# Two chunks of low parts on GpSimd and six on VectorE, in place of three and five, in two norms between stages

## The chip, the cores and the metric

One Trainium2 chip, one of its cores. The metric is the device time of one execution in microseconds (us). The engines are TensorE (PE, whose weight loads are listed apart as PEld), VectorE (DVE), ScalarE (ACT), GpSimd (POOL) and the queue that issues the weight loads from memory (SP).

## What is computed

Three blocks of a small network run one after the other on 256 tokens of width 1024: a mixer block with sparse attention and a gated feed-forward, a block with a convolution and Fourier mixer and a squared-ReLU feed-forward (this one also on 256 context tokens), and a block with neighbourhood attention and a squared-ReLU feed-forward. Between the stages stand norms with a shift and a gain that come from a conditioning vector:

```python
def _rms(x, g):
    xf = x.astype(jnp.float32)
    y = xf * lax.rsqrt(jnp.mean(xf * xf, axis=-1, keepdims=True) + EPS)
    return y.astype(x.dtype) * g

def _modulate(h, shift, scale):
    return h * (1 + scale) + shift
...
x = x + gx2 * _mlp(_modulate(_rms(x, norm_mlp_g[i]), sx2, cx2), mlp_w1[i], mlp_w2[i])
```

Two of these norms matter here: m0, ahead of the feed-forward of the second block, and na, ahead of the projection to queries, keys and values of the third. Both are made for 512 columns, 256 tokens and 256 context tokens side by side.

## The kernel before

**Split numbers.** A product in float32 is made of three products in a rounded format (fp32r): high part of the weights by high part of the activations, high weights by low activations, low weights by high activations. So each weight tile and each activation tile is held as a high part (a copy into fp32r) and a low part (what is left after the high part is subtracted). ScalarE copies the weights' high parts (whi, L1077), VectorE subtracts for their low parts (wlo, L1537).

**A norm that ends in split numbers.** The width of 1024 is eight chunks c = 0 to 7 of 128 partitions, each with two halves q of 256 columns. For m0 and na the order is:

1. VectorE makes the normed values of all eight chunks, half by half, into xn (L1996, 16 instructions). One operand, the inverse roots, lies in PSUM (ps[5]).
2. ScalarE adds the shift and rounds, into the high part Ahi (L1102, 16 instructions).
3. The low part is xn + shift - Ahi. GpSimd makes it for the chunks in LOW_P in two instructions a half: the subtraction (L2280, xn from xn and A) and the shift (L2282, A from xn). VectorE makes it for the other chunks in one instruction a half (L1988), after the sixteen of step 1.

```python
        def shifted_lo(st, layer, which):
            for c in LOW_P:
                for q in range(2):
                    x = xn[c][:, half(q)]
                    w.wait_ge(S(st + "_hi"), 2 * c + q + 1)
                    e.tensor_tensor(x, x, plain(Ahi[:, c, half(q)]), SUB).then_inc(own.sem, own.up())
                    w.wait_ge(own, own.n)
                    e.tensor_scalar(Alo[:, c, half(q)], x, 1.0, ada[:, layer, q, 24 * which + c:24 * which + c + 1],
                                    MUL, ADD).then_inc(S(st + "_lp").sem, 1)
```

**The first two output chunks of the next stage** (first_two, for w1_0a after m0 and for na_in after na). TensorE runs both outputs, here called tile 0 and tile 1, together over the high parts k = 0 to 7 (L589, L591), since these come one by one. Only then come the eight products with the low parts of tile 0, and then the eight of tile 1 (L595), in the order of k. Before each of tile 0, TensorE waits for both halves of low part k. Tile 0 is 512 columns wide in both stages, tile 1 is 512 in w1_0a and 256 in na_in. The other output chunks follow in `linear`, 24 matmuls each (L551, L563, L565). After na_in's tile 1 there stand first two more groups: head_sum (L950, which needs the squares that ScalarE makes of tile 0, L1469 and then L1472) and a sum for the modulation (L647).

**What each engine has behind these.** VectorE: the low parts of the weights of output chunks 2 and 3 (two times L1537), and in m0's stage two partial sums for the modulation (L1612). GpSimd: in w1_0a the squares and low parts of the hidden values (L2294, L2178), in na_in the Newton steps of the head norms (L2308). ScalarE: weights' high parts (L1077), then the outputs of tile 0 (L1367 in w1_0a). SP: loads of 512 KB into nine buffers (L474), in order, each waiting until TensorE has left the buffer that it fills.

The order of instructions on each engine is written out in the program and joined by semaphores. LOW_P sets the split on GpSimd, on VectorE and in TensorE's waits (ready_low, L606); the table IN_TURN holds how many signals each norm gives on a shared semaphore.

Of the kernel before, what the change touches and what calls it, by code (L numbers as in the profile page):

```python
# [48 lines left out]

AHEAD = {"w1_0a": 3, "na_in": 3}  # L50

LOW_P = range(3)
ADA_AFTER = {"w_in": (6, 22), "w_out": (0, 48), "w_up": (2, 42)}


# [149 lines left out]
def end_of(name):  # L205
# [6 lines left out]
                 ("d1_r", 8)],  # L212
    "normed": [("nc_t", 8), ("n2_t", 8), ("m0_t", 16), ("na_t", 16)],
    "norm_hi": [("nc_hi", 8), ("n2_hi", 8), ("m0_hi", 16), ("na_hi", 16)],
    "norm_lo": [("nc_lo", 8), ("n2_lo", 8), ("m0_lo", 10), ("na_lo", 10)],
    "norm_lo_p": [("m0_lp", 6), ("na_lp", 6)],
    "early_hi": [("e0_hi", 8), ("e1_hi", 8), ("e2_hi", 8)],
    "early_lo": [("e0_lo", 8), ("e1_lo", 8), ("e2_lo", 8)],
    "square": [("n1_sq", 8), ("nx_sq", 8), ("m0_sq", 8), ("na_sq", 8), ("m1_sq", 8)],
# [67 lines left out]
def launch_program(nc, dram, out):  # L287
# [222 lines left out]
    def tensor_program(e):  # L510
# [95 lines left out]
        def ready_low(v_signal, p_signal, per):  # L606

            def wait(k):
                if k in LOW_P:
                    w.wait_ge(S(p_signal), per * (k + 1))  # L610
                else:
                    w.wait_ge(S(v_signal), per * (k + 1 - len(LOW_P)))
            return wait
# [914 lines left out]
    def vector_program(e):  # L1528
# [455 lines left out]
        def shifted_lo(st, c, x, layer, which):  # L1984
            for q in range(2):
                w.wait_ge(S(st + "_hi"), 2 * c + q + 1)
                w.wait_ge(S(st + "_t"), 2 * c + q + 1)
                e.scalar_tensor_tensor(Alo[:, c, half(q)], x[:, half(q)], ada[:, layer, q, 24 * which + c:24 * which + c + 1],  # L1988
                                       plain(Ahi[:, c, half(q)]), ADD, SUB).then_inc(S(st + "_lo").sem, 1)

        def norm_whole(st, layer, which):

            for c in range(8):
                for q in range(2):
                    w.wait_ge(S(st + "_row"), 1)
                    e.scalar_tensor_tensor(xn[c][:, half(q)], R[:, c, half(q)], G[:, layer, which, q, c:c + 1], ps[5][:, half(q)],  # L1996
                                           MUL, MUL).then_inc(S(st + "_t").sem, 1)
            for c in range(len(LOW_P), 8):
                shifted_lo(st, c, xn[c], layer, which)
# [172 lines left out]
    def gpsimd_program(e):  # L2172
# [102 lines left out]
# [9 lines that stand above are left out]
# [205 lines left out]
```

## Time and profile before

| | us |
|---|---|
| median of 3 runs | 1355.67 |
| lowest and highest | 1353.74, 1355.76 |
| the profiled execution, its own time | 1354.78 |
| its span in the trace | 1352.6 |
| TensorE busy | 1318.6 (97%) |
| VectorE busy | 826.3 (61%) |
| ScalarE busy | 595.3 (44%) |
| GpSimd busy | 433.4 (32%) |

The span runs from the first to the last instruction in the trace; some 2 us lie around it. The granted clock of TensorE is given as a share of full speed: 1.00 is 2.4 GHz and 0.50 is 1.2 GHz. Each time below is one from the start of the span. The stage of m0 lies at about 575 us, that of na at about 945 us.

### The profile page before, as it was taken

The numbers are of one execution on the slowest core, as the hardware profiler recorded it, in microseconds if no ns is written. First come the engines' busy times: TensorE is split into PE (matmuls) and PEld (weight loads), VectorE is DVE, ScalarE is ACT, GpSimd is POOL, SyncE is SP. The second block draws the span as 40 slices with busy tenths as digits, with TensorE's granted clock in tenths as the row PEclk, the third lists the DMA queues.
The fourth block names the chain that finished last, engine by engine and source line by source line (L and its number), as shares of the span: only waits on it lengthen the run. The fifth ranks groups of instructions, "written<-read, shape, count | busy, mean of one in ns | idle before, by whom it ended". The sixth has DMA issues, their size and how long they took to land.

```text
span 1352.6 us, 19992 instructions
## 1 busy us (share of the span) xinstructions
PE 1318.6 (97%) x7852; PEld 1115.1 (82%) x7852; DVE 826.3 (61%) x1265; ACT 595.3 (44%) x953; POOL 433.4 (32%) x432
## 2 busy tenths in 40 slices
PE   9999999999999999979999999999799999999999
PEld 8888888899886788768788888787577777999987
DVE  6687678899776445369544444334467766855553
ACT  5336546566563223244321234222445553766432
POOL 2352132233420001265400144111556552388300
PEclk9999999999999999989999999999899999999999
DMA  7786367845455222344434333345423221555552
GB/s 288 264 280 235 142 210 277 300 181 182 162 189 193 78 94 79 111 153 160 167 128 152 143 140 140 140 142 185 161 89 108 93 84 45 187 188 181 188 191 79
DMA packets 63965, 220.08 MB, mean 163 GB/s; under 512 B 6913, under 2 KB 10241, under 8 KB 63873
## 3 DMA queue, kind: packets, MB, share of 16 engines
q1 hardware_dynamic: 63584, 218.56, 45.9%
q8 instruction: 63, 1.03, 0.3%
q10 hardware_dynamic: 288, 0.25, 0.1%
q14 instruction: 30, 0.24, 0.1%
HBM read 217.73 MB, written 1.05 MB: 162 GB/s over the span
## 4 chain that ended last, share of the span: by engine, by line
PE 89%; DVE 4%; POOL 3%; issue 2%; ACT 1%; DMA 1%; SPq 0%; DVEq 0%; POOLq 0%; ACTq 0%
PE ps L551 22%; PE ps L565 22%; PE ps L563 22%; PE ps L541 7%; PE ps L543 4%; PE ps L629 2%; POOL xn L2280 2%; PE ps L957 1%; PE ps L984 1%; PE ps L971 1%; DVE wlo L1537 1%; PE ps L595 1%; PE ps L950 1%; POOL ssum_c L2189 1%; DMA R<-in_x 1%
## 5 line engine op out<-in xcount | busy, mean ns | idle before, releaser
L551 PE MATMUL ps<-A,whi 128*128 128x256 f32 (+2 forms) x1580 | 519.3, 329 | 2.4 <-ACT A L1318 1.7
L565 PE MATMUL ps<-A,wlo 128*128 128x256 f32 (+2 forms) x1552 | 495.7, 319 | 0.1
L563 PE MATMUL ps<-A,whi 128*128 128x256 f32 (+2 forms) x1552 | 495.4, 319 | 0.0
L1537 DVE TENSOR_TENSOR wlo<-raw,whi 128x1024 fp32r<-128x1024 f32 x305 | 393.1, 1292 | 100.4 <-ACT whi L1077 100.1
L1077 ACT ACTIVATE whi<-raw 128x1024 fp32r<-128x1024 f32 x305 | 319.8, 1051 | 289.8 <-PE ps L565 163.0
L551 PEld LDWEIGHTS ps<-A,whi 128*128 128x128 f32 x1580 | 300.2, 190 | 55.9 <-issue 27.9
L563 PEld LDWEIGHTS ps<-A,whi 128*128 128x128 f32 x1552 | 295.2, 190 | 22.3 <-issue 1.9
L565 PEld LDWEIGHTS ps<-A,wlo 128*128 128x128 f32 x1552 | 294.7, 190 | 21.2 <-DVE wlo L1537 0.4
L541 PE MATMUL ps<-H,whi 128*128 128x512 f32 x432 | 151.4, 394 | 0.0
L2178 POOL TENSOR_TENSOR H<-tmp,H 128x256 fp32r<-128x256 f32 (+1 forms) x86 | 123.9, 1440 | 63.8 <-ACT H L1372 45.8
L543 PE MATMUL ps<-H,wlo 128*128 128x256 f32 x432 | 121.4, 281 | 0.0
L565 PE MATMUL ps<-H,wlo 128*128 128x512 f32 (+1 forms) x296 | 111.1, 375 | 0.6 <-DVE wlo L1537 0.6
L551 PE MATMUL ps<-H,whi 128*128 128x512 f32 (+1 forms) x296 | 111.5, 377 | 0.0
L563 PE MATMUL ps<-H,whi 128*128 128x512 f32 (+1 forms) x296 | 110.9, 375 | 0.0
L2294 POOL TENSOR_TENSOR tmp<-tmp 128x512 f32<-128x512 f32 (+1 forms) x64 | 56.0, 876 | 157.6 <-ACT tmp L1367 157.6
L541 PEld LDWEIGHTS ps<-H,whi 128*128 128x128 f32 x432 | 81.4, 188 | 18.1
L1961 DVE SCALAR_TENSOR_TENSOR R<-ps,ada,R 128x256 f32<-128x256 f32 x56 | 24.8, 479 | 114.9 <-PE ps L565 113.9
L2189 POOL TENSOR_TENSOR ssum<-ssum,sq 128x256 f32<-128x256 f32 (+1 forms) x30 | 32.0, 1067 | 170.7 <-ACT sq L1092 170.7
L543 PEld LDWEIGHTS ps<-H,wlo 128*128 128x128 f32 x432 | 82.1, 190 | 0.1
L551 PEld LDWEIGHTS ps<-H,whi 128*128 128x128 f32 x296 | 55.7, 188 | 11.7 <-issue 0.8
L565 PEld LDWEIGHTS ps<-H,wlo 128*128 128x128 f32 x296 | 55.7, 188 | 10.8 <-DVE wlo L1537 0.8
L563 PEld LDWEIGHTS ps<-H,whi 128*128 128x128 f32 x296 | 55.7, 188 | 9.9
(282 smaller groups left out, 1461.1 us busy)
## 6 DMA issues: line engine op xcount, KB each, us to landing
raw<-in_ada SPq DMA_DIRECT2D x96, 512.0 KB, 4.3
raw<-in_w SPq DMA_DIRECT2D x64, 512.0 KB, 3.4
raw<-in_w_up SPq DMA_DIRECT2D x44, 512.0 KB, 4.2
raw<-in_w_in SPq DMA_DIRECT2D x38, 512.0 KB, 5.5
raw<-in_w_0a SPq DMA_DIRECT2D x32, 512.0 KB, 3.6
raw<-in_w_0b SPq DMA_DIRECT2D x32, 512.0 KB, 3.4
raw<-in_na_in SPq DMA_DIRECT2D x24, 512.0 KB, 5.3
raw<-in_w_down SPq DMA_DIRECT2D x22, 512.0 KB, 3.4
```

The source lines that it names most:

```text
L541: e.matmul(ps[g % 3], w_hi, both(k), start=k == 0, stop=False)
L543: m = e.matmul(o, w_lo, ah, start=False, stop=last)
L551: e.matmul(o, w_hi, ah, start=k == 0, stop=False)
L563: e.matmul(o, w_hi, al, start=False, stop=False)
L565: m = e.matmul(o, w_lo, ah, start=False, stop=last)
L629: m = e.matmul(ps[7][q:q + 32, :], cond[:, k, :], raw[slot][:, 512 * j:512 * j + 512], start=k == 0 or i in (88, 89), stop=k == 7 and i < 48)
L1077: e.activation(whi[s % NHI][:, :cols], raw[i % NRAW][:, :cols], ACT.Copy).then_inc(S("whi").sem, 1)
L1537: e.tensor_tensor(wlo[i % NRAW][:, :cols], raw[i % NRAW][:, :cols], plain(whi[s % NHI][:, :cols]), SUB).then_inc(S("wlo").sem, 1)
L2178: e.tensor_tensor(into, x, plain(hi), SUB).then_inc(S(done).sem, 1)
L2189: e.tensor_tensor(total, total, x, ADD).then_inc(S(st + "_part").sem, 1)
L2280: e.tensor_tensor(x, x, plain(Ahi[:, c, half(q)]), SUB).then_inc(own.sem, own.up())
L2294: e.tensor_tensor(x, x, x, MUL).then_inc(S(st + "_sq").sem, 1)
```

## The change

GpSimd makes the low parts of chunks 0 and 1 in place of 0, 1 and 2, and VectorE those of chunks 2 to 7 in place of 3 to 7, in both norms. The counts of signals follow: two halves for each of the 6 chunks and 2 chunks.

```diff
-LOW_P = range(3)
+LOW_P = range(2)
...
-    "norm_lo": [("nc_lo", 8), ("n2_lo", 8), ("m0_lo", 10), ("na_lo", 10)],
-    "norm_lo_p": [("m0_lp", 6), ("na_lp", 6)],
+    "norm_lo": [("nc_lo", 8), ("n2_lo", 8), ("m0_lo", 12), ("na_lo", 12)],
+    "norm_lo_p": [("m0_lp", 4), ("na_lp", 4)],
```

On VectorE, in the norm m0 (xn_126 is the normed chunk 2, xn_127 chunk 3, and so on; "x2" is the two halves), the difference of the orders reads:

```order
 L1996 SCALAR_TENSOR_TENSOR xn_130<-R,G,ps 128x256 x2
 L1996 SCALAR_TENSOR_TENSOR xn_131<-R,G,ps 128x256 x2
+L1988 SCALAR_TENSOR_TENSOR A<-xn_126,ada,A 128x256 x2
 L1988 SCALAR_TENSOR_TENSOR A<-xn_127,ada,A 128x256 x2
 L1988 SCALAR_TENSOR_TENSOR A<-xn_128,ada,A 128x256 x2
```

Two instructions are put ahead of the ten, so each of those, and what stands behind them, comes two places later; the same two rows are added in na. On GpSimd, in the norm m0 (tmp_87 is the first hidden tile of the stage that follows):

```order
 L2280 TENSOR_TENSOR xn_125<-xn_125,A 128x256
 L2282 TENSOR_SCALAR A<-xn_125,ada 128x256
-L2280 TENSOR_TENSOR xn_126<-xn_126,A 128x256
-L2282 TENSOR_SCALAR A<-xn_126,ada 128x256
-L2280 TENSOR_TENSOR xn_126<-xn_126,A 128x256
-L2282 TENSOR_SCALAR A<-xn_126,ada 128x256
 L2294 TENSOR_TENSOR tmp_87<-tmp_87 128x512
 L2178 TENSOR_TENSOR H<-tmp_87,H 128x512
```

The last four of its twelve instructions for this norm are gone, and the same four in na. The rows of TensorE, ScalarE and SP are the same before and after.

## Rows read from the trace of the kernel before

**Rows 1.** The page: busy time, share of the span and instructions of each engine.

```profile
PE 1318.6 (97%) x7852; PEld 1115.1 (82%) x7852; DVE 826.3 (61%) x1265; ACT 595.3 (44%) x953; POOL 433.4 (32%) x432
```

**Rows 2.** TensorE's waits, whole span: total us, times, longest.

```profile
PE ps L595 <- POOL A L2282: 12.7, 2, 6.5
...
PE ps L589 <- ACT A L1102: 1.7, 2, 0.8
```

**Rows 3.** Timeline of GpSimd, 566 to 602 us: start, us, what.

```profile
576.19 0.73 POOL L2280 TENSOR_TENSOR xn<-xn,A 128x256 f32<-128x256 f32 x1 [8.63 <-ACT A L1102]
...
580.92 0.48 POOL L2282 TENSOR_SCALAR A<-xn,ada 128x256 fp32r<-128x256 f32 x1
581.37 6.89 POOL L2280 TENSOR_TENSOR xn<-xn,A 128x256 f32<-128x256 f32 x1
...
590.38 0.48 POOL L2282 TENSOR_SCALAR A<-xn,ada 128x256 fp32r<-128x256 f32 x1
```

**Rows 4.** Timeline of VectorE, 566 to 602 us.

```profile
581.36 4.04 DVE L1988 SCALAR_TENSOR_TENSOR A<-xn,ada,A 128x256 fp32r<-128x256 f32 x10
585.32 2.35 DVE L1537 TENSOR_TENSOR wlo<-raw,whi 128x1024 fp32r<-128x1024 f32 x2
587.59 2.10 DVE L1612 TENSOR_SCALAR modsum<-raw,cond 128x1024 f32<-128x1024 f32 x2
```

**Rows 5.** Timeline of TensorE, 566 to 602 us.

```profile
583.92 0.39 PE L591 MATMUL ps<-A,wlo 128*128 128x512 f32 x1
584.14 0.61 PE L595 MATMUL ps<-A,whi 128*128 128x512 f32 x2
590.91 6.29 PE L595 MATMUL ps<-A,whi 128*128 128x512 f32 x14 [6.15 <-POOL A L2282]
597.04 0.39 PE L551 MATMUL ps<-A,whi 128*128 128x512 f32 x1
```

**Rows 6.** Timeline of GpSimd, 936 to 972 us.

```profile
951.43 6.86 POOL L2280 TENSOR_TENSOR xn<-xn,A 128x256 f32<-128x256 f32 x1
...
959.66 0.48 POOL L2282 TENSOR_SCALAR A<-xn,ada 128x256 fp32r<-128x256 f32 x1
```

**Rows 7.** Timeline of VectorE, 936 to 972 us.

```profile
951.39 4.04 DVE L1988 SCALAR_TENSOR_TENSOR A<-xn,ada,A 128x256 fp32r<-128x256 f32 x10
```

**Rows 8.** Timeline of TensorE, 936 to 990 us.

```profile
947.39 0.28 PE L589 MATMUL ps<-A,whi 128*128 128x256 f32 x1
947.50 0.28 PE L591 MATMUL ps<-A,wlo 128*128 128x256 f32 x1
...
953.05 0.63 PE L595 MATMUL ps<-A,whi 128*128 128x512 f32 x2
960.19 4.63 PE L595 MATMUL ps<-A,whi 128*128 128x512 f32 x14 [6.51 <-POOL A L2282]
964.62 1.53 PE L950 MATMUL ps<-sq,con 128*128 128x512 f32 x2
...
967.08 0.50 PE L551 MATMUL ps<-A,whi 128*128 128x512 f32 x1
...
983.40 1.02 PE L950 MATMUL ps<-sq,con 128*128 128x512 f32 x2
```

**Rows 9.** Timeline of ScalarE, 936 to 972 us.

```profile
963.16 0.60 ACT L1469 ACTIVATE k<-ps 128x512 f32<-128x512 f32 x1 [9.06 <-PE ps L595]
963.65 0.59 ACT L1472 ACTIVATE sq<-ps 128x512 f32<-128x512 f32 x1
```

**Rows 10.** Stretches: us, busy time and count of each engine, granted clock, DMA share, GB/s.

```profile
670.00:760.00 90.00, 90.00 (x407) 73.07 (x407) 34.85 (x41) 18.44 (x19) 3.64 (x3) 1.00 0.39 141
590.90:597.20 6.30, 6.29 (x15) 4.97 (x16) 0.00 (x0) 0.60 (x1) 1.04 (x1) 0.52 0.26 86
960.20:965.00 4.80, 4.80 (x15) 4.18 (x16) 0.00 (x0) 1.09 (x2) 0.00 (x0) 0.50 0.16 55
```

**Rows 11.** Timeline of SP's loads, 560 to 640 us: the second of the two issues last.

```profile
573.60 20.60 SPq L474 DMA_DIRECT2D raw<-in_w_0a  x2
```

## Prediction

> **What bounds the kernel now.** I read the page first: TensorE is busy 1318.6 of 1352.6 us [rows 1], so a change gains or loses by what it does to TensorE's idle time and to its clock, and by nothing else. The list of TensorE's waits comes next. Its longest entry is exactly the place that the change touches: L595, the products with the activations' low parts, waits 12.7 us in two pieces for GpSimd's L2282 [rows 2]. That is over a third of the 34 us in which TensorE is idle at all (1352.6 - 1318.6).
>
> The timelines of the two stages say why. In the first stage GpSimd's subtraction and shift of a half take 0.73 and 0.48 us and follow each other at 1.30 us a half, four times. The fourth ends at 581.40 (580.92 + 0.48). The fifth subtraction, the first half of chunk 2, starts at 581.37 and takes 6.89 us in place of 0.73 [rows 3]. What began then is VectorE's chain of low parts, at 581.36, with two L1537 right behind it and two L1612 after those, with no gap from 581.36 to 589.69 [rows 4]. The subtraction ends at 588.26, which is 0.59 us after the last L1537 (587.67). In the second stage the same subtraction starts at 951.43 and takes 6.86 us [rows 6], again in step with VectorE's chain, which begins at 951.39 [rows 7]. So the subtraction is shut out for as long as VectorE runs instructions with both tensors in SBUF back to back. It isn't shut out by L1996, whose second tensor is in PSUM: beside these the first subtraction took its 0.73 us [rows 3].
>
> The Trainium skill bears on this ("SBUF — State Buffer", section "Who interferes with whom"): a VectorE instruction with two SBUF inputs contends with a GpSimd instruction that reads SBUF, and who issues first holds the shared pair for the whole instruction. On who contends, the trace agrees (6.89 against 0.73 us). On how long, it doesn't: by a hold of one instruction the subtraction would get its turn after 0.4 us, and the waits of 6.15 and 6.51 us would hardly be there; the sum would then be next to nothing, or slightly a loss, since VectorE gets two more instructions.
>
> TensorE meanwhile does low products 0 and 1 at 584.14 and stops; it goes on at 590.91, 0.05 us after the last L2282 [rows 3, 5]. The pause also costs clock. The fourteen products left take 6.13 us (590.91 to 597.04), 0.44 each, against 0.23 for one of this width just before (583.92 to 584.14) [rows 5]. The granted clock over them is 0.52, which is 1.2 GHz nearly throughout, and 0.50 in the second stage, against 1.00, or 2.4 GHz, in steady work [rows 10].
>
> **The change part by part: the first stage.** GpSimd loses four instructions, all behind the point at which it was shut out; its first eight stand as before and end at 581.40. VectorE gets two L1988 ahead of its ten. The ten take 4.04 us with 0.48 for one, so they start (4.04 - 0.48) / 9 = 0.396 us apart [rows 4]. Twelve of them, counted j = 0 to 11, end at 581.36 + 0.396 j + 0.48; chunk k is done with j = 2(k - 2) + 1. TensorE wants chunk k at 584.14 + 0.227 k. Chunk 2 is ready at 582.24 and wanted at 584.60, chunk 5 is ready at 584.61 and wanted at 585.28, chunk 6 ready at 585.41 and wanted at 585.51: no wait. Chunk 7 is ready at 586.20, with the 0.05 us of signal 586.25, and wanted at 585.73: a wait of 0.5 us. Tile 0 ends at 586.48, tile 1 takes 8 x 0.227 = 1.82 and ends at 588.30. There the next output chunk begins, which stood at 597.04 [rows 5]. Gain: 8.7 us. Seen otherwise, 6.15 of wait less 0.5, and 3.0 of slow clock.
>
> **The second stage.** VectorE's chain starts at 951.39 [rows 7] and TensorE's low products at 953.05 [rows 8], 1.66 us after it and not 2.78 as in the first, so here VectorE is the later one. Chunks 2, 3 and 4 come in time (chunk 4 at 953.90, wanted at 953.96). Chunk 5 comes at 954.69 against 954.19, chunk 6 at 955.48, chunk 7 at 956.28: three waits of about 0.5 us, and tile 0 ends at 956.51. Tile 1 is 256 wide, 0.115 us each (947.39 to 947.50) [rows 8]: 0.92, to 957.43. L950 needs ScalarE's squares of tile 0. Before, tile 0 ended at about 960.19 + 6 x 0.44 = 962.83 (its last six products at half clock, each as in the first stage), and ScalarE started at 963.16, 0.33 later; the squares end 1.08 after that (963.65 + 0.59 - 963.16) [rows 9]. Now: 956.51 + 0.33 + 1.08 = 957.92, with the signal 957.97, a new wait of 0.5 us, formerly hidden behind tile 1 at half clock. From L950 to the next output chunk it was 967.08 - 964.62 = 2.46; L950 itself took 1.53 at the slow clock and 1.02 at the fast one, so 0.51 less: 1.95. The next output chunk begins at 959.92 in place of 967.08 [rows 8]. Gain: 7.2 us.
>
> **What else moves.** VectorE's two L1537 come 0.79 us later. The first ended at about 586.5 and now at 587.3, and TensorE wants it near 588.5 in the first stage: a cover of 1.2 us, and without it the stage would give back that much at most. GpSimd's first hidden square may now meet VectorE's chain (tile 0 is out at about 587.3, the chain with L1612 runs to 590.5) and be held up to 3 us; the hidden tiles are read only in the next product, over 70 us later, from a ring of five, so this is free. The loads: SP issued nothing from 574 to 594 and then waited on TensorE's tile 0 [rows 11], so nothing was fetched in the pause that will now be missing; these loads move forward with TensorE. The first of them is for output chunk 4, which TensorE wants two chunks (2 x 24 x 0.227 = 10.9 us) after chunk 2 begins: before at 607.9, 13.7 us behind the issue at 594.2, and now at 599.2, 12.7 us behind an issue at 586.5. One us of cover goes, since tile 1 runs at full clock, out of 13.7.
>
> **The sum.** 8.7 + 7.2 = 15.9 us. From the profiled execution's own 1354.78 that makes 1338.9 us. The median of the runs is 1355.67, 0.9 us more; I stay with the profiled one.
>
> **The bounds of what no row shows** concern the clock: whether it stays up through the three short waits in the second stage: at best nothing is lost; at worst what [rows 10] show is paid again after them (tile 1 and the last of tile 0 1.1 us, L950 0.5, and some of the next chunk, 3 us in all a stage, 6 in both). I take nothing, since the waits are 0.5 us each and TensorE already waits 0.8 us ahead of each stage's first product [rows 2] and runs the products behind that wait at 0.115 us for 256 columns, full speed [rows 8]. Upward the bound is that VectorE's twelve cost no wait at all: the waits of 6.15 and 6.51 and the slow clock, 3.0 in the first stage and in the second (964.62 - 960.19) - 6 x 0.227 - 8 x 0.115 + 0.51 = 2.7: 18.4 us, so 1336.4.
>
> **The rivals.**
> - *The clock falls in the stutter.* Up to 3 us in one stage or both: 1342 to 1345. Against it: full clock in the 90 us of steady work, and 0.8 us waits that cost nothing.
> - *Given back later.* Something after the stages is tied to time rather than to TensorE, such as a load or a norm chain. At half of the gain: 1347. For it: the attention stage has small waits of its own; against: SP's loads follow TensorE, and ScalarE had idled for 9.06 us when it got tile 0 [rows 9], so it brought no debt into the stage that follows.
> - *GpSimd is still caught.* The margin is thin: the eighth instruction ends at 581.40, VectorE's chain begins at 581.36 [rows 3, 4]. If the fourth pair is caught, it is let go at 588.26 + 0.79 = 589.05, its rest takes 0.6, and TensorE goes on at 589.7 from product 1 (15 left, 0.44 more): 0.8 us gained a stage, 1353.2. Nothing ahead of this point is altered, and both stages got through before.
> - *Slower: GpSimd is caught three pairs early.* Then the second pair is let go at 589.05, its shift takes 0.6 and two pairs follow at 1.3: chunk 1 is done at 592.25, against 590.86 for chunk 2 before, and one product more runs at half clock: 1.8 us lost a stage, 1358.5. With only the third and fourth caught it is 590.95 and 0.5 us lost a stage, 1355.9, so it decides from there on. It takes GpSimd 2.6 to 3.9 us later, or VectorE's chain that much earlier, and sixteen L1996 still stand ahead of it.
> - *The hold is one of a single instruction, and TensorE's wait has another cause.* Then VectorE's 0.79 us more a stage is all there is: 1356.4, within the measurement. Against it: TensorE goes on 0.05 us after L2282.
>
> **How the numbers follow.** Forecast 0.80 (its own range 1336.4 to 1341), clock 0.07, given back 0.06, GpSimd still caught 0.03, no hold 0.02, slower 0.02. The predicted time is 1338.9. The range takes in the clock rival and the upper bound with 0.9 us for the spread of the runs: 1335.5 to 1345. A measurement of this kernel tells 0.2%, 2.7 us, from no change. Faster by more: forecast, clock, given back and a part of the rest, 0.94; within 0.2%: 0.04; slower: 0.02.
>
> **What the profile after would show.** Right: no L2280 longer than 0.8 us, twelve L1988 in about 4.84 us, L595 waiting for VectorE's L1988 (about 0.5 us once in the first stage, 0.5 three times in the second), L595's products at 0.23 us, a clock of 1.00 in both, L950 waiting for ScalarE some 0.5 us, the next output chunk at about 588.3 and 951.2 (959.9 less 8.7). Wrong: a subtraction of over 6 us among GpSimd's eight, a clock of 0.50 behind the stutter, or a new entry of several us in TensorE's waits after 590 us.

## The result, and the profile after

| | before | after |
|---|---|---|
| median, us | 1354.7 (4 runs) | 1336.78 (4 runs) |
| lowest and highest | 1352.75, 1355.76 | 1336.65, 1338.93 |
| the profiled execution, own time | 1354.78 | 1338.93 |
| its span | 1352.6 | 1337.0 |

The changed kernel is 1.3% faster: ratio 0.9873, 95% interval 0.9856 to 0.989. The forecast was 1338.9 us.

The page after, busy times:

```profile
PE 1314.3 (98%) x7852; PEld 1111.0 (83%) x7852; DVE 825.1 (62%) x1269; ACT 595.9 (45%) x953; POOL 417.3 (31%) x424
```

Against [rows 1], GpSimd is busy for 16 us less, of which 12.3 are the time that two subtractions were held (6.89 - 0.73 and 6.86 - 0.73); TensorE is busy for 4.3 us less, mostly since its products no longer run at half clock there.

TensorE's waits after, longest first (total us, times, longest):

```profile
PE ps L675 <- POOL ssum_c L2189: 1.9, 1, 1.9
PE ps L551 <- ACT A L1318: 1.7, 3, 1.4
PE ps L711 <- ACT whi L1077: 1.5, 1, 1.5
PE ps L595 <- DVE A L1988: 1.2, 4, 0.3
```

The entry of 12.7 us [rows 2] is gone. In its place L595 waits for VectorE, four times, 1.2 us in all by this list; from start to start it is 2.2 us, as worked out below. First stage, timelines of GpSimd, VectorE and TensorE after (this execution is 1.29 us later than that of before where the norm begins, 576.38 against 575.09 for the first L1996):

```profile
577.48 0.73 POOL L2280 TENSOR_TENSOR xn<-xn,A 128x256 f32<-128x256 f32 x1 [8.64 <-ACT A L1102]
...
581.34 0.74 POOL L2280 TENSOR_TENSOR xn<-xn,A 128x256 f32<-128x256 f32 x1
582.18 0.48 POOL L2282 TENSOR_SCALAR A<-xn,ada 128x256 fp32r<-128x256 f32 x1
588.77 1.89 POOL L2294 TENSOR_TENSOR tmp<-tmp 128x512 f32<-128x512 f32 x1 [6.11 <-ACT tmp L1367]
```

```profile
576.38 6.36 DVE L1996 SCALAR_TENSOR_TENSOR xn<-R,G,ps 128x256 f32<-128x256 f32 x16 [0.76 <-PE ps L692]
582.65 4.84 DVE L1988 SCALAR_TENSOR_TENSOR A<-xn,ada,A 128x256 fp32r<-128x256 f32 x12
587.40 2.36 DVE L1537 TENSOR_TENSOR wlo<-raw,whi 128x1024 fp32r<-128x1024 f32 x2
```

```profile
585.41 1.84 PE L595 MATMUL ps<-A,whi 128*128 128x512 f32 x7
587.55 2.36 PE L595 MATMUL ps<-A,whi 128*128 128x512 f32 x9 [0.29 <-DVE A L1988]
589.75 0.40 PE L551 MATMUL ps<-A,whi 128*128 128x512 f32 x1
```

GpSimd's last shift still ends 0.01 us past the start of VectorE's chain (582.66 and 582.65) and isn't held. Seven low products run without a stop where two did [rows 5], then one gap: the eighth would start at 585.41 + 7 x 0.227 = 587.00 and starts at 587.55. The figure in brackets, 0.29, is smaller, since a matmul's span reaches past the start of the next. The hidden square L2294 met the chain and took 1.89 us; nothing waited for it. Second stage, TensorE:

```profile
945.76 1.35 PE L595 MATMUL ps<-A,whi 128*128 128x512 f32 x5
947.39 0.50 PE L595 MATMUL ps<-A,whi 128*128 128x512 f32 x1 [0.29 <-DVE A L1988]
948.19 0.50 PE L595 MATMUL ps<-A,whi 128*128 128x512 f32 x1 [0.29 <-DVE A L1988]
948.98 1.46 PE L595 MATMUL ps<-A,whi 128*128 128x512 f32 x9 [0.29 <-DVE A L1988]
950.66 1.13 PE L950 MATMUL ps<-sq,con 128*128 128x512 f32 x2 [0.22 <-ACT sq L1472]
...
952.71 0.50 PE L551 MATMUL ps<-A,whi 128*128 128x512 f32 x1
```

Three gaps while VectorE brings chunks 5, 6 and 7, and one ahead of L950. The stretches of both stages after (last three columns: granted clock, DMA share, GB/s) show full clock throughout, against 0.52 and 0.50 [rows 10]:

```profile
584.10:588.30 4.20, 3.90 (x17) 2.86 (x16) 4.20 (x10) 1.42 (x3) 0.00 (x0) 1.00 0.00 0
588.30:598.00 9.70, 9.70 (x44) 7.98 (x44) 8.96 (x8) 4.63 (x7) 5.98 (x4) 1.00 0.86 302
943.00:951.00 8.00, 6.91 (x33) 4.97 (x32) 8.00 (x17) 4.88 (x9) 1.06 (x2) 1.00 0.08 10
```

A yardstick for all runs below: the length of a stage from the first L1996 of its norm to the first L551 behind L595, read from the two timelines. Here it is 589.75 - 576.38 = 13.37 and 952.71 - 937.82 = 14.89 us; before it was 597.04 - 575.09 = 21.95 and 967.08 - 945.12 = 21.96.

### The profile page after: what moved, and what is told of

Its sections match the earlier page's. It is cut to its first block, busy times and chain, and to the rows that moved or that the text cites. A ratio compares the mean times of both kernels' runs of the same rounds, so it can differ in the third digit from the quotient of the medians.

```text
span 1337.0 us, 19992 instructions
## 1 busy us (share of the span) xinstructions
PE 1314.3 (98%) x7852; PEld 1111.0 (83%) x7852; DVE 825.1 (62%) x1269; ACT 595.9 (45%) x953; POOL 417.3 (31%) x424
## 4 chain that ended last, share of the span: by engine, by line
PE 89%; DVE 5%; ACT 2%; issue 2%; POOL 1%; DMA 1%; SPq 0%; DVEq 0%; POOLq 0%; ACTq 0%
PE ps L551 23%; PE ps L565 22%; PE ps L563 22%; PE ps L541 7%; PE ps L543 4%; PE ps L629 2%; PE ps L957 1%; PE ps L984 1%; PE ps L971 1%; DVE wlo L1537 1%; ACT A L1102 1%; PE ps L950 1%; DVE A L1988 1%; POOL ssum_c L2189 1%; DMA R<-in_x 1%
## 5 line engine op out<-in xcount | busy, mean ns | idle before, releaser
L551 PE MATMUL ps<-A,whi 128*128 128x256 f32 (+2 forms) x1580 | 519.3, 329 | 2.3 <-ACT A L1318 1.7
L565 PE MATMUL ps<-A,wlo 128*128 128x256 f32 (+2 forms) x1552 | 495.9, 320 | 0.1
L563 PE MATMUL ps<-A,whi 128*128 128x256 f32 (+2 forms) x1552 | 495.8, 319 | 0.0
L1537 DVE TENSOR_TENSOR wlo<-raw,whi 128x1024 fp32r<-128x1024 f32 x305 | 388.6, 1277 | 92.0 <-ACT whi L1077 91.4
L551 PEld LDWEIGHTS ps<-A,whi 128*128 128x128 f32 x1580 | 300.3, 190 | 55.3 <-issue 25.9
L563 PEld LDWEIGHTS ps<-A,whi 128*128 128x128 f32 x1552 | 295.6, 190 | 22.0 <-issue 1.7
L565 PEld LDWEIGHTS ps<-A,wlo 128*128 128x128 f32 x1552 | 295.1, 190 | 21.4 <-DVE wlo L1537 0.4
L565 PE MATMUL ps<-H,wlo 128*128 128x512 f32 (+1 forms) x296 | 111.1, 375 | 0.6 <-DVE wlo L1537 0.6
L551 PE MATMUL ps<-H,whi 128*128 128x512 f32 (+1 forms) x296 | 111.5, 377 | 0.0
L563 PE MATMUL ps<-H,whi 128*128 128x512 f32 (+1 forms) x296 | 111.0, 375 | 0.0
L2294 POOL TENSOR_TENSOR tmp<-tmp 128x512 f32<-128x512 f32 (+1 forms) x64 | 58.3, 911 | 159.1 <-ACT tmp L1367 158.9
L551 PEld LDWEIGHTS ps<-H,whi 128*128 128x128 f32 x296 | 55.7, 188 | 11.6 <-issue 0.8
L565 PEld LDWEIGHTS ps<-H,wlo 128*128 128x128 f32 x296 | 55.7, 188 | 10.9 <-DVE wlo L1537 0.8
L563 PEld LDWEIGHTS ps<-H,whi 128*128 128x128 f32 x296 | 55.7, 188 | 9.9
```

Source lines behind the costliest of these rows:

```text
L551: e.matmul(o, w_hi, ah, start=k == 0, stop=False)
L563: e.matmul(o, w_hi, al, start=False, stop=False)
L565: m = e.matmul(o, w_lo, ah, start=False, stop=last)
L1537: e.tensor_tensor(wlo[i % NRAW][:, :cols], raw[i % NRAW][:, :cols], plain(whi[s % NHI][:, :cols]), SUB).then_inc(S("wlo").sem, 1)
L2294: e.tensor_tensor(x, x, x, MUL).then_inc(S(st + "_sq").sem, 1)
```

## The experiments

Each was timed beside the kernel before, on three chips: runs 1 to 4, 5 to 7 and 8 to 10. All lengths are of the one profiled execution of each kernel. The expected times start from the medians of the first series, and the kernel before is 0.8 to 2.8 us lower on these chips, so a median is best read against "before, same chip".

| kernel | stage 1, us | stage 2, us | median, us | before, same chip | ratio, 95% interval |
|---|---|---|---|---|---|
| before | 21.95 | 21.96 | | | |
| the change | 13.37 | 14.89 | 1336.78 | 1354.7 | 0.9873, 0.9856 to 0.989 |
| 1 GpSimd first | 15.19 | 17.84 | 1343.31 | 1351.89 | 0.9932, 0.9909 to 0.9954 |
| 2 gaps | 16.65 | 17.76 | 1341.83 | 1351.89 | 0.9926, 0.99 to 0.9951 |
| 3 m0 alone | 13.34 | 21.38 | 1345.96 | 1351.89 | 0.9949, 0.9931 to 0.9967 |
| 4 na alone | 20.81 | 14.89 | 1343.99 | 1351.89 | 0.9945, 0.9923 to 0.9966 |
| 5 one chunk | 14.12 | 15.68 | 1339.97 | 1353.87 | 0.9895, 0.9878 to 0.9913 |
| 6 no chunk | 14.92 | 16.48 | 1342.55 | 1353.87 | 0.9915, 0.9898 to 0.9933 |
| 7 GpSimd late | 19.50 | 20.72 | 1352.46 | 1353.87 | 0.9991, 0.9978 to 1.0004 |
| 8 the change again | 13.33 | 14.89 | 1339.76 | 1353.34 | 0.99, 0.9881 to 0.9919 |
| 9 in turns | 12.64 | 14.88 | 1338.39 | 1353.34 | 0.989, 0.9871 to 0.991 |
| 10 in turns, sum first | 12.67 | 13.40 | 1337.94 | 1353.34 | 0.9879, 0.986 to 0.9899 |

**1. GpSimd first.** Is the subtraction shut out by VectorE, or slow by itself?

```diff
+            w.wait_ge(S(st + "_lp"), 6)
             for c in range(len(LOW_P), 8):
                 shifted_lo(st, c, xn[c], layer, which)
```

> The split of before (three chunks on GpSimd, five on VectorE), but VectorE waits ahead of its first L1988 until GpSimd has made all six halves. Theory 1, GpSimd is shut out by VectorE's chain: its fifth subtraction takes 0.73 us as the first four, the six halves are done 2.6 us after the fourth, VectorE's ten follow, TensorE's last low part is some 1.9 us later than with the change. Stage one gains 6.9 us and stage two 5.2 us against before: about 1342.6 us, clock 1.00 throughout. Theory 2, the fifth subtraction is slow for another reason (its data, TensorE's or ScalarE's reads of A): it takes 6.9 us again and VectorE only starts then, over 4 us lost a stage, above 1360 us.

GpSimd's fifth and sixth half, and VectorE behind them, in the first stage (L2281, L2283 are L2280, L2282 of before):

```profile
582.65 0.74 POOL L2281 TENSOR_TENSOR xn<-xn,A 128x256 f32<-128x256 f32 x1
583.49 0.48 POOL L2283 TENSOR_SCALAR A<-xn,ada 128x256 fp32r<-128x256 f32 x1
583.94 0.74 POOL L2281 TENSOR_TENSOR xn<-xn,A 128x256 f32<-128x256 f32 x1
584.77 0.48 POOL L2283 TENSOR_SCALAR A<-xn,ada 128x256 fp32r<-128x256 f32 x1
```

```profile
585.29 4.05 DVE L1988 SCALAR_TENSOR_TENSOR A<-xn,ada,A 128x256 fp32r<-128x256 f32 x10 [2.54 <-POOL A L2283]
```

The same instruction on the same data takes 0.74 us when VectorE rests, so theory 2 falls. A wait of 2.54 us put into VectorE makes the kernel faster. Stage one gained 6.76 us (6.9 expected), stage two 4.12 (5.2 expected); there the granted clock was 0.50 for some 3 us from 953.3 us on, behind six short waits of TensorE for low parts, which I hadn't reckoned with.

**2. Gaps.** How long does the hold last?

```diff
                 w.wait_ge(S(st + "_t"), 2 * c + q + 1)
+                if c > 3 or q:
+                    w.wait_ge(S(st + "_lo"), 2 * (c - 3) + q)
                 e.scalar_tensor_tensor(Alo[:, c, half(q)], ...
```

> The split of before, but each L1988 of VectorE waits until the one before it is written, so that VectorE stands still for a moment between them. Theory 1a, GpSimd is shut out only as long as VectorE's instructions overlap without a gap: the fifth subtraction gets in after one or two L1988 and takes under 2 us, the ten L1988 take 5.8 us alone and some 2 us more with GpSimd's between them, the gain is some 5 us in stage one and 4 in stage two: 1344 to 1348 us. Theory 1b, VectorE goes first whenever both want it: the subtraction lasts to the end of the chain, now 1.5 us later or more, 1356 to 1360 us.

GpSimd and VectorE in the first stage (L2282 is the subtraction here, L2284 the shift, L1990 VectorE's low part):

```profile
579.87 1.08 POOL L2282 TENSOR_TENSOR xn<-xn,A 128x256 f32<-128x256 f32 x1
581.06 0.53 POOL L2284 TENSOR_SCALAR A<-xn,ada 128x256 fp32r<-128x256 f32 x1
581.56 0.90 POOL L2282 TENSOR_TENSOR xn<-xn,A 128x256 f32<-128x256 f32 x1
582.56 0.53 POOL L2284 TENSOR_SCALAR A<-xn,ada 128x256 fp32r<-128x256 f32 x1
```

```profile
579.88 6.57 DVE L1990 SCALAR_TENSOR_TENSOR A<-xn,ada,A 128x256 fp32r<-128x256 f32 x10
```

Of the ten, the second by itself:

```profile
580.49 0.75 DVE L1990 SCALAR_TENSOR_TENSOR A<-xn,ada,A 128x256 fp32r<-128x256 f32 x1
```

Theory 1a holds. Two of VectorE's ten, the second and the fourth, started while a subtraction ran and took 0.75 us; the others took 0.48. So the ten start (6.57 - 0.48 - 2 x 0.27) / 9 = 0.62 us apart, not counting those 0.27 us, and leave 0.14 us between them, where before each began at 0.396 us, ahead of the end of the one in front (0.48 long). That is enough: the subtraction took 1.08 us beside the chain, not 6.89 [rows 3], and the two engines took turns.

The stages gained 5.3 and 4.2 us, and that with a slow clock: the granted clock was 0.50 from 586.7 to 590.1 and from 951.9 to 955.3 us. The last nine products of the first stage took 3.75 us (586.50 to 590.25) where 9 x 0.227 = 2.04 would do at full clock, so the gaps alone would be worth some 1.7 us more there (an estimate). The median of 1341.83 lies 2.2 us below the range expected; before is 2.8 us lower on this chip than on the first.

**3 and 4. One norm alone.** LOW_P by norm: two chunks for one, three for the other, with the counts of signals to match.

> Two chunks on GpSimd in the norm m0 alone, three in na as before. If the two stages pay independently and nothing is given back, the 8.6 us that the trace shows between the norm's first L1996 and the next output chunk: 1346.1 us. If what is gained in one place is given back later, clearly above that, and this run and the next don't add up to the whole.

> Two chunks on GpSimd in the norm na alone, three in m0 as before. Independent stages: the 7.1 us that the trace shows for this stage, 1347.6 us. Given back in the attention stage behind it: clearly above.

The changed stage has the same length alone as with the other (13.34 and 13.37, 14.89 and 14.89), and the stretch between the stages is 348.1 us in every kernel of the table. Behind the second stage, from its first L551 to the end of the span, it is 384.3 or 384.4 us with the change and in runs 1 to 6 and 9; in the other four (before 385.5, run 7 387.0, run 8 385.7, run 10 387.3) the clock fell somewhere in that stretch. So the two gains are independent and none is given back. The medians, 5.9 and 7.9 us below before, add up to 13.8, less sharply than the stages do; run 4 came out 3.6 us below its expectation, 1.1 of it in the stage that it left as it was. The stage left as it was came out at 20.81 and 21.38 here, not 21.95 and 21.96, with the same wait: the part at half clock varied.

**5 and 6. One chunk, no chunk on GpSimd.** The change with LOW_P one and zero chunks long.

> One chunk on GpSimd and seven on VectorE in both norms. If TensorE now waits only for the end of VectorE's chain, two more L1988 at 0.396 us put that 0.79 us later in each stage: 1.6 us slower than the change, about 1338.4 us. If the two chunks that GpSimd makes hold TensorE or VectorE back (the thin margin), it is no slower, or faster: 1336.8 us or less.

> No chunk on GpSimd, all eight on VectorE. By the same reckoning the chain ends 1.58 us later than with the change in each stage: 3.2 us slower than the change, about 1340.0 us, and still 15 us faster than before. If GpSimd's share were what makes the difference between before and after, and not the shutting out, this would be slower than before.

The stages got longer by 0.75 and 0.79 us for one chunk and by 1.55 and 1.59 us for none: 0.79 us a chunk, two L1988, as expected. So after the change TensorE waits for the end of VectorE's chain, and GpSimd's two chunks are worth 3.1 us in all. The medians came out 1.6 and 2.6 us above what was expected; the changed kernel itself moved as much from one chip to another (run 8). GpSimd with three chunks is worse than with none at all.

**7. GpSimd late.** How near is the edge?

```diff
                     w.wait_ge(S(st + "_hi"), 2 * c + q + 1)
+                    if c and q:
+                        e.tensor_scalar(xn[0][:, half(0)], xn[0][:, half(0)], 1.0, 0.0, MUL, ADD).then_inc(own.sem, own.up())
+                        w.wait_ge(own, own.n)
                     e.tensor_tensor(x, x, plain(Ahi[:, c, half(q)]), SUB).then_inc(own.sem, own.up())
```

> The change, with one idle instruction of 0.48 us more on GpSimd ahead of the subtraction of its fourth half (on a tile that nobody needs any longer), so that this half's shift falls 0.1 us behind the start of VectorE's chain. Theory 1, the fourth half is caught: its L2282 ends at the end of VectorE's L1537 pair, TensorE stops after product 0 for some 5 us, 15 products run at half clock in the first stage, 13.7 us of the gain are lost in the two stages: about 1350.5 us (within 3 us, by when the clock falls). Theory 2, the shift (one SBUF input, one scalar) is not shut out as the subtraction is, or a delay of 0.5 us is just that: 1336.8 to 1337.5 us.

The added instruction (L2281), the last subtraction and the last shift of GpSimd, and VectorE's chain:

```profile
581.00 0.41 POOL L2281 TENSOR_SCALAR xn<-xn 128x256 f32<-128x256 f32 x1
581.49 0.75 POOL L2283 TENSOR_TENSOR xn<-xn,A 128x256 f32<-128x256 f32 x1
582.34 7.99 POOL L2285 TENSOR_SCALAR A<-xn,ada 128x256 fp32r<-128x256 f32 x1
```

```profile
582.29 4.83 DVE L1988 SCALAR_TENSOR_TENSOR A<-xn,ada,A 128x256 fp32r<-128x256 f32 x12
587.04 2.35 DVE L1537 TENSOR_TENSOR wlo<-raw,whi 128x1024 fp32r<-128x1024 f32 x2
589.32 1.55 DVE L1612 TENSOR_SCALAR modsum<-raw,cond 128x1024 f32<-128x1024 f32 x2
```

Theory 1 holds. The shift began 0.05 us behind VectorE's chain and took 7.99 us. It has one SBUF tensor to read and was held no less than the subtraction: until 590.33, which is 0.9 us after the last L1537. In the second stage it took 7.38 us. The stages lost 6.1 and 5.8 us of the gain, 11.9 in all where 13.7 were expected, since the granted clock was 0.50 for a shorter time than I had taken (590.5 to 593.9 and 955.7 to 962.5 us, against 586.8 to 597.0 in the first stage before). The median of 1352.46 can't be told from before. The margin that the change lives on is about half a microsecond of GpSimd's time.

**8 to 10. Tile 0 and tile 1 in turns.** With the chain's end as the limit, TensorE can fill its gaps with tile 1, and put L647 ahead of L950.

```diff
-            for s, Tn, o in tiles:
-                for k in range(8):
-                    lo_ready(k)
+            for k in range(8):
+                lo_ready(k)
+                for s, Tn, o in tiles:
                     m = e.matmul(o, whi[s % NHI][:, 128 * k:128 * k + 128], acts(k)[1][:, :Tn], start=False, stop=k == 7)
-                m.then_inc(S("mm").sem, 1)
+                    if k == 7:
+                        m.then_inc(S("mm").sem, 1)
...
+            if n == 1:
+                mod_summed("na_in", n)
             if 0 <= m < 24:
                 if norm2(m):
```

The second part, and the guard of the old call by `n != 1`, are in run 10 alone.

> The changed kernel once more, for comparison with the next two on the same chip: 1336.8 us as before.

> The changed kernel, and the low products of tile 0 and tile 1 taken in turns for each k, so that tile 1's fill the waits for VectorE. First stage: sixteen products of 0.227 us from 585.4 us on are longer than the chain's rest, the 0.57 us gap goes. Second stage: tile 1 ends 0.12 us behind tile 0 and no longer 0.9 us, but L950 waits for ScalarE's squares of tile 0, which come no earlier: nothing. 1336.2 us. If L950's wait isn't what counts there, another 0.8 us less: 1335.4 us.

> The same with the modulation's sum L647 put ahead of the head sum L950 behind na_in's tile 1, so that its 1.0 us lies in the wait for the squares: another 1.1 us in the second stage, 1335.2 us. If the longer way of L950 to VectorE's head mean is on the path of what follows, less or nothing.

In the first stage the turns gained 0.69 us (0.57 expected), in the second nothing by themselves, as expected. With the sum moved the yardstick says 1.49 us there (1.1 expected), but its end has moved too. TensorE in run 10, second stage (L648 and L951 are L647 and L950 of before):

```profile
944.53 2.25 PE L595 MATMUL ps<-A,whi 128*128 128x512 f32 x12
946.94 0.62 PE L595 MATMUL ps<-A,whi 128*128 128x512 f32 x2 [0.16 <-DVE A L1992]
947.73 0.62 PE L595 MATMUL ps<-A,whi 128*128 128x512 f32 x2 [0.18 <-DVE A L1992]
948.28 1.07 PE L648 MATMUL ps<-modsum,pick 128*32 128x512 f32 x8
949.40 1.12 PE L951 MATMUL ps<-sq,con 128*128 128x512 f32 x2
949.97 0.79 PE L551 MATMUL ps<-A,whi 128*128 128x512 f32 x1
950.60 0.40 PE L563 MATMUL ps<-A,whi 128*128 128x512 f32 x1
```

The first L551 stands right behind the head sum here and takes 0.79 us, not 0.50, and the L563 behind it starts 0.63 us later, not 0.34 (953.05 - 952.71 with the change). Measured to that L563 the stage is 950.60 - 936.57 = 14.03 us long, against 953.05 - 937.82 = 15.23 with the change: 1.20 us gained.

By the medians, 1337.94 stands against 1339.76 for run 8 on the same chip, but the ranges touch (1335.92 to 1339.32, 1339.25 to 1340.52) and the intervals of the ratios overlap. The 1.9 us (0.69 and 1.20) are shown in the trace and not settled by the time of the whole kernel. Run 8, the same program as the change, took 3.0 us more than the 1336.8 expected: the mean granted clock of its four executions was 0.996 or 0.997, and in three of the four of the first series it was 1.000.

## Why the prediction was right

- **What bounds the kernel.** Right: the wait of 12.7 us and the slow clock behind it are gone, and the two stages are 15.65 us shorter.
- **Who shuts GpSimd out.** Right: run 1 takes VectorE's chain away from beside GpSimd and the subtraction takes 0.74 us, run 7 puts a shift under the chain and it takes 7.99. The weighing against the rule also stood: the hold lasted for the chain, not for one instruction. What the prediction only said in passing, "back to back", is the point: with 0.14 us between VectorE's instructions GpSimd gets its turn (run 2).
- **First stage.** 8.7 us forecast, 21.95 - 13.37 = 8.58 measured. The wait for chunk 7 was put at 0.5 us and is 0.55.
- **Second stage.** 7.2 us forecast, 21.96 - 14.89 = 7.07 measured. Three gaps of about 0.5 us: 0.49, 0.57 and 0.56 from start to start. L950's wait of 0.5: tile 1 ends at 948.98 + 0.227 + 8 x 0.115 = 950.13 and L950 starts at 950.66.
- **The sum.** 15.9 forecast; 15.65 in the stages, 15.6 in the spans. The profiled execution after took 1338.93 us, so near to the forecast partly by luck: with the change the clock fell once more ahead of the first stage (near 161 us, 1.3 us), and before it fell once more behind the second (near 996 us, 1.2 us), and the two cancel. The medians are 17.9 apart, since the execution profiled after is the slowest of its four (clock 0.997, the others 1.000); on the chip of run 8 they are 13.6 apart. The forecast's 15.9 stands between.
- **The covers.** The L1537 brought no wait in L565 or L551. The hidden square was held (1.89 against 1.04 us) for free, as said. No wait of TensorE's behind the stages grew.
- **The clock rival** didn't come true in these stages, but it was a fair one: the clock fell in the second stage of run 1, which lost about a microsecond against its sum, and in both stages of run 2. Run 6 has six short waits in its second stage, as run 1 has, and kept the full clock. So the runs don't show which stutter costs the clock, and "I take nothing" was a bet that held.
- **Given back later** didn't come true: the stretches between and behind the stages are as long as before, but for the places where the clock fell (runs 3 and 4).
- **The rivals "a hold of a single instruction" and "slower"** didn't come true either: the stages gained 15.65 us, and with the change no subtraction of GpSimd's took over 0.75 us.
- **The rival that GpSimd is still caught** was priced at 1353.2 us, and run 7, which brings it about, has a median of 1352.46. Nothing ahead of this point was altered, and GpSimd finished in time again; half a microsecond more would have been enough to lose nearly the whole gain.

## What to carry to other kernels

Before work is given to GpSimd to relieve VectorE, look at what VectorE runs at that moment: here a GpSimd instruction that started just behind the start of an unbroken chain of VectorE instructions with two tensors in SBUF ended only after that chain (0.3 to 0.9 us after it). So GpSimd's share is best done before the chain begins, or be none. In the trace this shows as one GpSimd instruction many times as long as its like, starting with VectorE's chain and ending behind it. If the share can't be moved, a break between VectorE's instructions lets GpSimd in and can pay although VectorE gets slower (run 2, 5.3 and 4.2 us).

## What the runs showed of the hardware

- **The hold belongs to the gapless chain.** Instructions of 0.48 us that start 0.396 us apart, with two of 1.22 us right behind them, shut GpSimd out for 6.9 to 8.0 us; the same ones 0.62 us apart, with 0.14 us between them, cost it 0.35 us (1.08 against 0.73). The Trainium skill ("SBUF — State Buffer", section "Who interferes with whom") speaks of a hold for one instruction. Run 2 agrees with it, and both ways: VectorE's instruction took 0.75 us when it began while a subtraction ran. Among overlapping instructions of this kind the runs show GpSimd getting no turn.
- **Behind the chain, VectorE and GpSimd slow each other and neither is shut out.** L1612 reads one tensor of 128x1024 from SBUF and follows the last L1537 with no gap [rows 4], yet before, the held subtraction got through as it began (it ended at 588.26). GpSimd's next shift and subtraction took 0.79 and 1.15 us beside the two L1612; in the second stage, where VectorE rested, they took 0.48 and 0.73. The two L1612 took 1.21 and 0.97 us; three others in the same execution, with GpSimd idle, took 0.74 or 0.75.
- **Outside the stages, the profiled executions differ by TensorE's clock at a few places far from the change.** Two executions of the same changed kernel, the same stretches (columns as in [rows 10]), first the one shown above, then run 8:

```profile
160.00:166.00 6.00, 5.26 (x32) 5.13 (x31) 3.38 (x7) 2.38 (x6) 0.26 (x1) 0.72 0.27 101
...
1130.00:1145.00 15.00, 13.09 (x104) 11.51 (x103) 11.15 (x18) 9.12 (x17) 3.56 (x4) 1.00 0.43 151
```

```profile
160.00:166.00 6.00, 4.86 (x38) 4.66 (x39) 4.01 (x8) 3.88 (x7) 1.02 (x2) 1.00 0.41 146
...
1130.00:1145.00 15.00, 13.09 (x93) 11.51 (x92) 11.04 (x17) 8.42 (x17) 3.51 (x4) 0.89 0.40 141
```

  In the profiled executions the clock fell near 11, 161, 366 and 1134 to 1137 us in some and not in others, the same program too (before and run 7 also near 996 and 993 us, run 7 near 1150 us). The stretch behind the second stage is 384.3 us long where it doesn't fall there (the changed kernel: 1337.0 - 952.71) and 1338.5 - 952.8 = 385.7 in run 8 where it does. Among the four executions of the first series the span goes with the mean granted clock as well: 1337.0 us at 0.997, 1334.8 to 1334.9 at 1.000. A gain of one or two us in this kernel is therefore read from a stage and not from the whole.
- **The clock outlived the same stop for different times.** Before, TensorE stopped at 584.8 and the clock fell at 586.8; in the second stage it stopped at 953.7 and the clock fell at about 958.8. When it comes back differs too: before, in the first stage, at about 597.0, and in run 4, with the same wait and the same code there, at about 592.8. So the price of a stop of 6 us differed by a microsecond between executions (stage one 21.95 and 20.81 us).
